# Dense FFN up and gate products as seven products of halves instead of eight; modulation weights in four slots

## The reference

```python
def swiglu(x, w1, w3, w2):
    return (jax.nn.silu(x @ w1) * (x @ w3)) @ w2
...
    cond = jax.nn.silu(c)
...
        mod = (cond @ w_mod[l] + b_mod[l])[:, None, :]
        sh_a, sc_a, g_a, sh_f, sc_f, g_f = jnp.split(mod, N_MOD, axis=-1)
...
        x = x + g_f * ((jax.nn.silu(h @ w_gate[l]) * (h @ w_up[l])) @ w_down[l])
```

## Time and profile before

| | |
|---|---|
| median of 3 runs | 2234.43 us (2232.43 to 2234.75) |
| profiled execution, its own time | 2232.85 us |
| its span | 2231.1 us |
| TensorE (PE) matmul busy | 2116.5 us, 95% |
| TensorE weight load (PEld) busy | 1525.7 us, 68% |
| DVE busy | 658.6 us, 30% |
| ACT busy | 363.8 us, 16% |

### The profile page before, as it was taken

The page is one execution under the profiler, slowest core; times in us unless marked ns, Lnnn a source line. Parts: engine busy times, 40 slices in busy tenths (PEclk is TensorE's granted clock), DMA queues, the critical chain, the costliest instruction groups (busy, mean ns, idle before and its releaser), DMA issues.

```text
span 2231.1 us, 33975 instructions
## 1 busy us (share of the span) xinstructions
PE 2116.5 (95%) x14688; PEld 1525.7 (68%) x14688; DVE 658.6 (30%) x1635; ACT 363.8 (16%) x861; POOL 83.7 (4%) x180
## 2 busy tenths in 40 slices
PE   8998999999989999998999999899999998999998
PEld 7786776777678877855643553487677757867776
DVE  1415424333334154242010000244433333440001
ACT  1312230000013122300010000133200012430000
POOL 3000000000000000020000000000000020000000
PEclk9999999999999998998999999999999999999999
DMA  8333234688563342337999999942579763224442
GB/s 254 114 96 123 95 123 151 210 274 285 173 193 105 93 139 82 123 97 248 348 313 371 345 323 364 298 133 95 177 232 306 255 183 113 96 95 151 134 149 94
DMA packets 333817, 421.23 MB, mean 189 GB/s; under 512 B 27222, under 2 KB 282148, under 8 KB 333668
## 3 DMA queue, kind: packets, MB, share of 16 engines
q1 hardware_dynamic: 312464, 352.96, 49.1%
q0 software_dynamic: 13408, 50.66, 6.8%
q10 hardware_dynamic: 7796, 15.43, 2.0%
HBM read 417.90 MB, written 1.05 MB: 188 GB/s over the span
## 4 chain that ended last, share of the span: by engine, by line
PE 87%; DVE 4%; ACT 3%; issue 2%; DMA 2%; ACTq 1%; POOL 0%; DVEq 0%; POOLq 0%
PE psum L1255 31%; PE psum L1372 10%; PE psum L1262 9%; PE psum L1273 9%; PE psum L1432 5%; PE psum L1889 3%; PE psum L1502 2%; PE psum L1673 2%; PE psum L1291 2%; PE psum L1361 1%; PE psum L1700 1%; PE psum L1445 1%; DVE arena L2061 1%; ACTq L635 1%; DMA arena<-in_w_mod 1%
## 5 line engine op out<-in xcount | busy, mean ns | idle before, releaser
L1255 PE MATMUL psum<-xT,ring 128*128 128x256 f32 x3520 | 786.4, 384 | 3.9 <-ACT small L758 2.1
L1255 PEld LDWEIGHTS psum<-xT,ring 128*128 128x128 f32 x3520 | 672.5, 192 | 118.9 <-issue 20.5
L1273 PE MATMUL psum<-ring,arena 128*128 128x512 f32 x528 | 232.8, 594 | 0.0
L1262 PE MATMUL psum<-ring,xT 128*128 128x256 f32 (+2 forms) x960 | 205.5, 373 | 11.8 <-DVE arena L2300 4.4
L1262 PEld LDWEIGHTS psum<-ring,xT 128*128 128x128 f32 x960 | 174.4, 194 | 39.9 <-DVE arena L2300 5.7
L1273 PEld LDWEIGHTS psum<-ring,arena 128*128 128x128 f32 x528 | 100.3, 191 | 114.9 <-issue 112.5
L2072 DVE TENSOR_TENSOR arena<-arena,psum 128x512 f32<-128x512 f32 x33 | 22.7, 687 | 407.4 <-PE psum L1255 235.0
L2061 DVE SCALAR_TENSOR_TENSOR arena<-arena,cond 128x256 f32<-128x256 f32 x336 | 135.0, 478 | 0.0
L1372 PE MATMUL psum<-ring,arena 128*32 128x256 f32 x2304 | 126.9, 379 | 0.7 <-DVE arena L2144 0.7
L667 ACT ACTIVATE arena<-psum 128x512 f32<-128x512 f32 x33 | 19.7, 597 | 578.2 <-PE psum L1255 571.9
L1372 PEld LDWEIGHTS psum<-ring,arena 128*32 128x32 f32 x2304 | 74.6, 110 | 51.3 <-issue 3.4
(11 more groups left out here) (392 smaller groups left out, 1865.5 us busy)
## 6 DMA issues: line engine op xcount, KB each, us to landing
ring<-in_w_in SPq DMA_DIRECT2D x80, 1024.0 KB, 5.4
ring<-in_exp_w SPq DMA_DIRECT2D x312, 256.0 KB, 6.0
arena<-in_w_mod POOLq DMA_DIRECT2D x48, 1024.0 KB, 10.1
ring<-in_ffn_w SPq DMA_DIRECT2D x33, 1024.0 KB, 6.1
arena<-in_exp_w SPq DMA_DIRECT2D x120, 256.0 KB, 6.8
ring<-in_w_gate SPq DMA_DIRECT2D x22, 1024.0 KB, 7.7
ring<-in_w_up SPq DMA_DIRECT2D x22, 1024.0 KB, 10.1
ring<-in_w_down SPq DMA_DIRECT2D x22, 1024.0 KB, 5.1
```

The source lines that it names most:

```text
L1255: ins = pe.matmul(dst, w[:, k * 256 + c0:k * 256 + c0 + m], act_t[:, k, :], start=(k == 0), stop=(k == KT - 1))
L1262: ins = pe.matmul(dst, act_t[:, k, t * P:t * P + P], w[:, k * 256 + c0:k * 256 + c0 + n], start=(k == 0), stop=(k == KT - 1))
L1273: ins = pe.matmul(psum[:, 4 + 2 * t + h, :], gT[:, s % 3, f * 256 + t * P:f * 256 + t * P + P], w2[:, f * D + h * 512:f * D + h * 512 + 51 ...
```

## The change

**The products.** In steps 1 to 10 of every dense FFN `xT` is cut into four quarters (channel half x token tile) and each of `w1`, `w3` into two channel halves. The outputs h1 and h3 of both token tiles are then a 2x2 times 2x2 product of blocks. It is made by seven products instead of eight (`product`: 8 matmuls with 128 moving tokens each), of which five take sums or differences. `token_sums` makes four sums of quarters of `xT` once per FFN (`xsum`, in the space of `oT`); `weight_sums` makes four sums of halves of `w1` and `w3` per step, one step ahead, on DVE (one overwrites half of the `w3` unit in the ring). The products are put together on DVE by four additions (C11, a half-width one, C22, C21) in `hh`, with one copy of the first product on ACT; then come Silu and the multiplication as before. The `down` products are unchanged.

**The modulation.** Four slots instead of three; a load waits for the unit four before. DVE's operations are cut into 19 pieces of about 10 operations, two pieces in a step (behind C21 and behind g), the last behind g of step 9. `add_mod` is one piece that stands after token tile 0's last `down` and ahead of tile 1's.

**Elsewhere.** `angles` moves up on DVE to behind the last merged block ahead of the residual; the three Sin move up on ACT accordingly.

```diff
+FIRST_BANK, PAIR_BANK, SIDE_BANK, LAST_BANK = 2, 3, 0, 1
...
+        mod_slots = [modw[:, i, :] for i in range(3)] + [view(SLOT, at=8192 - SLOT)]
...
                 for j in range(MOD_UNITS):
-                    if j >= 3:
-                        pool.wait_ge(*ready("dve", "mod", l, j - 3))
+                    if j >= 4:
+                        pool.wait_ge(*ready("dve", "mod", l, j - 4))
...
             def dense(key):
-                for s in range(FFN_STEPS):
-                    act.wait_ge(*ready("pe_job", "h1", *key, s))
+                act.wait_ge(*ready("pe_job", "h1", *key, 0))
+                step(act.activation(hh[:, 0:2, :], two(psum[:, 0, :]), ACT.Silu), "silu", *key, 0)
+                for s in range(1, FFN_STEPS):
+                    act.wait_ge(*ready("pe_job", "P1", *key, s))
                     if s >= 2:
-                        act.wait_ge(*ready("dve", "g", *key, s - 2))
-                    step(act.activation(sil[:, s % 2, :], psum[:, (2 * s) % 4, :], ACT.Silu), "silu", *key, s)
+                        act.wait_ge(*ready("dve", "C11", *key, s - 1))
+                    step(act.copy(part[:], psum[:, FIRST_BANK, 0:UNIT_FF]), "P1", *key, s)
+                    act.wait_ge(*ready("dve", "C21", *key, s))
+                    step(act.activation(hh[:, 0:2, :], hh[:, 0:2, :], ACT.Silu), "silu", *key, s)
...
+            def product(bank, half, weights, tokens):
+
+                for f in range(2):
+                    dst = psum[:, bank, half * 256 + f * P:half * 256 + f * P + P]
+                    for k in range(4):
+                        ins = pe.matmul(dst, weights[:, k, f * P:f * P + P], tokens[:, k, :],
+                                        start=(k == 0), stop=(k == 3))
+                return ins
...
+                    w1, w3 = [unit(key, w, s).rearrange("p (k c) -> p k c", k=KT) for w in ("w1", "w3")]
+                    if s >= 2:
+                        pe.wait_ge(*ready("act", "P1", *key, s - 1))
+                    job(product(FIRST_BANK, 0, w1[:, 0:4, :], x11), "P1", *key, s)
+                    if s >= 2:
+                        pe.wait_ge(*ready("dve", "C11", *key, s - 1))
+                    product(PAIR_BANK, 0, w1[:, 4:8, :], x21)
+                    pe.wait_ge(*ready("dve", "xsums", *key))
+                    pe.wait_ge(*ready("dve", "wsums", key, s))
+                    job(product(PAIR_BANK, 1, wsum2, xsum[:, 1]), "P26", *key, s)
+                    used(key, "w1", s)
...
+                    product(SIDE_BANK, 1, w3[:, 0:4, :], xsum[:, 2])
+                    job(product(SIDE_BANK, 0, wsum1, xsum[:, 0]), "P75", *key, s)
+                    pe.wait_ge(*(ready("dve", "C21", *key, s - 1) if s >= 2 else ready("dve", "g", *key, 0)))
+                    product(LAST_BANK, 1, w3[:, 4:8, :], xsum[:, 3])
+                    job(product(LAST_BANK, 0, wsum4, x22), "P34", *key, s)
+                    used(key, "w3", s)
+                    if s < last:
+                        downed(down(key, s - 1, w2), key, s - 1)
+                    else:
+                        down(key, s - 1, w2, (0,))
+                    w2_old, w2 = w2, unit(key, "w2", s)
+                job(down(key, last, w2, (0,)), "sum", *key)
                 if key in MOD_HOME:
-                    add_mod(MOD_HOME[key], 0)
...
+                    add_mod(MOD_HOME[key])
+                downed(down(key, last - 1, w2_old, (1,)), key, last - 1)
+                downed(down(key, last, w2, (1,)), key, last)
...
+            def weight_sums(key, s):
+
+                for w in ("w1", "w3"):
+                    dve.wait_ge(*ready("slot%d" % ring_place[key, w, s], "unit", key, w, s))
+                w1, w3 = [ring[:, ring_place[key, w, s], :].rearrange("p (k c) -> p k c", k=KT) for w in ("w1", "w3")]
+                if s >= 2:
+                    dve.wait_ge(*ready("pe_job", "P75", *key, s - 1))
+                step(dve.tensor_tensor(wsum1[:], w3[:, 0:4, :], w3[:, 4:8, :], ALU.add))
+                free(dve.tensor_tensor(w3[:, 0:4, :], w1[:, 0:4, :], w3[:, 0:4, :], ALU.subtract))
+                step(dve.tensor_tensor(wsum2[:], wsum1[:], w1[:, 0:4, :], ALU.subtract))
+                if s >= 2:
+                    dve.wait_ge(*ready("pe_job", "P34", *key, s - 1))
+                free(dve.tensor_tensor(wsum4[:], w1[:, 4:8, :], wsum2[:], ALU.subtract), "wsums", key, s)
...
+                for s in range(1, FFN_STEPS):
+                    dve.wait_ge(*ready("act", "P1", *key, s))
+                    dve.wait_ge(*ready("pe_job", "P26", *key, s))
...
+                    if s + 1 < FFN_STEPS:
+                        weight_sums(key, s + 1)
+                    dve.wait_ge(*ready("pe_job", "P34", *key, s))
+                    step(dve.tensor_tensor(hh[:, 1:3, :], hh[:, 1:3, :], two(psum[:, LAST_BANK, :]), ALU.add),
+                         "C21", *key, s)
+                    if s + 1 < FFN_STEPS:
+                        some_modulation(2 * s - 1)
                     dve.wait_ge(*ready("act", "silu", *key, s))
...
+                    some_modulation(2 * s)
```

More of the change, by code:

```diff
@@ L923, in _ @@
                     step(act.activation(zb[:, :, c, :], zb[:, :, c, :], ACT.Sigmoid), "sig", l, c)
+                if l == 0:
+                    act.wait_ge(*ready("dve", "angles"))
+                    for side, sign in ((0, -1.0), (1, 1.0)):
+                        step(act.activation(trig_sin[:, :, side, :], two(ang[:, 1, :]), ACT.Sin, scale=sign))
+                    step(act.activation(trig_cos[:], two(ang[:, 2, :]), ACT.Sin), "trig")
                 warm_roots("ln1", l)
@@ L934, in _ @@
                     step(act.activation(e2, e2, ACT.Exp), "router_exp")
-                if l == 0:
-                    act.wait_ge(*ready("dve", "angles"))
-                    for side, sign in ((0, -1.0), (1, 1.0)):
-                        step(act.activation(trig_sin[:, :, side, :], two(ang[:, 1, :]), ACT.Sin, scale=sign))
-                    step(act.activation(trig_cos[:], two(ang[:, 2, :]), ACT.Sin), "trig")
                 if l == 0:
@@ new lines, in token_sums @@
+            def token_sums(key):
+                x11, x12, x21, x22 = [xT[:, 4 * (i // 2):4 * (i // 2) + 4, P * (i % 2):P * (i % 2) + P]
+                                      for i in range(4)]
+                if key[0] == "ffn1":
+                    dve.wait_ge(*ready("act", "xt", "f1", 0, 1))
+                else:
+                    dve.wait_ge(*ready("act", "modulated", "ffn", key[1], 1))
+                    dve.wait_ge(*ready("dve", "modulated", "ffn", key[1], 1))
+                step(dve.tensor_tensor(xsum[:, 0], x12, x11, ALU.subtract))
+                free(dve.tensor_tensor(xsum[:, 2], x22, x12, ALU.subtract))
+                step(dve.tensor_tensor(xsum[:, 1], x22, xsum[:, 0], ALU.subtract))
+                free(dve.tensor_tensor(xsum[:, 3], x21, xsum[:, 1], ALU.subtract), "xsums", *key)
```

130 lines of the change are left out of this document (67 added, 63 removed).

## The result

| | before | after |
|---|---|---|
| median, same chip | 2234.75 us (5 runs, 2232.43 to 2242.83) | 2226.88 us (5 runs, 2224.74 to 2229.54) |
| ratio | | 0.9949, 95% interval 0.9929 to 0.9969 |
| profiled execution, its own time | 2232.85 us | 2229.54 us |
| its span, mean granted clock | 2231.1 us, 0.981 | 2227.8 us, 0.971 |

The change makes the kernel faster by 0.5%, where 0.7% was forecast. The median lies 9 us above the forecast of 2218 and inside the range of 2195 to 2228, near its end.

What follows compares the result with a forecast made beforehand. TensorE's matmuls, busy 95% of the span, were taken as the bound. 34.7 - 20.0 - 3.3 + 5.1 = 16.5 us off 2232.85 gave 2216.4, plus 1.58 for a median: 2218 us, range 2195 to 2228.

Steps and rivals of the forecast that it cites:

- products, three FFNs: Steps 1 to 10 of each dense FFN: 56 short matmuls replace 32 of 256 columns, saving 34.7 us.
- gaps in the steps: Two FFNs with modulation: TensorE waits for late weight sums and g, costing 20.0 us, bounds 0 and 26.
- clock behind these gaps: After two of the four stalls the granted clock falls, 1.64 us each: 3.3 us lost, bounds 0 and 6.6.
- the ends: Ends of the first two FFNs, up to the next stage's transposes: 2.1 and 3.0 us gained, 5.1 together.
- Two pairs in one step: In step 3, 4 MB of modulation makes w3 land at 22.7 us; TensorE waits 4.6 us, twice per FFN.
- At no cost: In the FFN steps DVE's load, token sums, ACT's copy and Silu, and moved angles cost nothing.
- No stalls: Rival: the two pairs' loads fall apart or yield to the ring's; 39.8 us gained, 2194.6 us, chance 0.32.
- stalls of 2 us: If DMA queues share the rate equally, the second pair delays w3 by about half; stalls 2 us, not 4.6.
- More stalls: Rival: two pairs meet the weights in every third step and gaps cost clock; 2232 to 2236 us, chance 0.08.
- Slower by a new bound: Rival: weights land late in every step with modulation; 2278 us if w3 always lands at 22.7, chance 0.07.

Runs made afterwards that it cites:

- run 9: The changed kernel measured a second time, unaltered, against the kernel before: 2225.07 us against 2237.98 us, ratio 0.9940.
- Experiment 1: Changed kernel with modulation loads held back until the w3 unit of the step behind the pair's first operation has landed: 2209.81 us, ratio 0.9871 to the kernel before.
- experiment 2: Changed kernel loading only the first four of 24 modulation units per layer, DVE's work kept: 2202.4 us, ratio 0.9824 to the kernel before.
- experiment 5: Changed kernel with modulation cut into pieces of 16, then 4 and 5 in turn, so pairs begin one step apart: 2207.89 us, ratio 0.9846 to the kernel before.
- experiment 3: Changed kernel with all modulation loads but only the first and last of DVE's eight multiply-adds per unit: one run of 2222.39 us.
- experiment 7: Changed kernel with modulation cut 14, then 4 and 5, its loads held behind w3, and add_mod between tile 0's last down groups: 2190.01 us, ratio 0.9776 to the kernel before.
- experiments 6: Changed kernel with add_mod between token tile 0's two last down groups instead of behind them: 2215.77 us, ratio 0.9887 to the kernel before.
- experiment 4: Changed kernel with three slots for modulation units instead of four: 2282.55 us, ratio 1.0192 to the kernel before.

## Why the prediction was right, and where it was off

The sum was 16.5 us. Against the second profile of the kernel before, which has the changed kernel's clock outside the FFNs, the span fell by 13.0 (2240.8 to 2227.8), and by 12.9 in the medians of run 9. Step by step:

| us | forecast | measured |
|---|---|---|
| products, three FFNs | +34.7 | +39.3 (30 x 1.31) |
| gaps in the steps | -20.0 | -20.1 |
| clock behind these gaps | -3.3 | -6.1 |
| the ends | +5.1 | +3.2 |
| clock behind the ends | not counted | -4.1 |
| sum | 16.5 | 12.2 |

The number came close partly by luck: the products gave 4.6 us more than forecast, the clock and the ends took 8.8 more, and within the gaps step 4 was shorter and step 8 longer than said. The steps that were mis-sized are these.

- **The products** were mis-sized, for the better. 12.51 us for 56 is 0.2234 us each, not 0.2266 or 0.2256. The 7.25 us of step 0 in the earlier trace rows run from the first matmul after an idle of 1.16, so what a start behind an idle costs was spread over only 32 matmuls; a group of 16 records behind a gap takes 1.86 us start to start (508.08), 1.79 within the stream. The rate within a long stream was 1.2% better, and over 1680 matmuls that is 4.6 us. The 81 ns of the Trainium skill (TensorE: Matmul & The Clock Gate, section Back-to-back issue gap) would have been 324 ns a matmul by the prediction's working; the trace has 223.4, so the page's figure does not hold for this stream. Short matmuls did not slow down over 56 in a row.
- **Two pairs in one step** was right in place and, in the sum, in size: the large gaps are in steps 4 and 8 of both FFNs. Their sum is 2.75 + 0.36 + 5.33 + 0.29 + 1.11 = 9.8 in the first and 0.27 + 2.28 + 5.44 + 1.23 + 1.11 = 10.3 in the second (0.36, 0.29 and 0.27 are small gaps in steps 6, 10 and 3), where 10.0 was said. Experiments 1, 2 and 5 show the cause, and experiment 3 that less work on DVE does not take it away. The inner course was only partly as told. In step 4 the last link was DVE's queue, which stood 6.6 us for modulation where some 4 were said; in step 8 it was `w3` itself, 25 us after its step's start where 22.7 was said. TensorE waited for it at the step's start and not only ahead of the third product, since its program asks for `w1` and `w3` both before the first product. Doubling the delay of one pair was 2 us too little: seven units of 1.05 MB in a step of 19.4 us would be 379 GB/s, more than the 320 and 367 that the first two windows below show at a DMA share of 0.96 and 1.02. So the load of two pairs does not end within its step, and by the packet counts above it is the ring's that ends last.
- **The clock.** Two falls of 1.64 were taken; three came in the steps, of 1.69, 1.80 and 2.63, within the bound of 6.6. But the two in step 8 hide a wait. There the weight sums for the third product ended at 552.42 + 1.22 = 553.64 us, and TensorE came to it at 554.19. At full clock it would have come at 548.82 + 3.57 = 552.39 and waited for DVE until about 553.8 (at 467.12 it started 0.15 after the sums' end). So that fall cost about 0.4 us and not 1.80, and by the same working on the second FFN's rows 1.2 and not 2.63 (estimates from these starts). Experiment 1 shows the case: behind 2.37 us idle nothing fell (3.81 us at 540.73), and 1.16 of waiting for DVE followed. So the clock's own price in the steps is an estimated 3.3 us, and the late `w3` costs some 2.8 more than the row of gaps says, 22.9: the term that was mis-sized is the landing of `w3` in step 7, at 25 us in place of 22.7. Windows of the changed kernel (as in experiment 7; the last three figures are granted clock, DMA share and GB/s): the step with two pairs, the start of the next with its gap, then behind this gap, and last in step 8 when the clock was back:

```profile
441.00:460.00 19.00, 19.00 (x128) 15.38 (x128) 12.38 (x25) 0.89 (x2) 3.51 (x4) 1.00 0.96 320
...
460.00:466.00 6.00, 4.37 (x34) 3.73 (x32) 5.83 (x8) 0.00 (x0) 0.00 (x0) 1.00 1.02 367
...
467.00:471.00 4.00, 3.88 (x20) 3.92 (x21) 3.96 (x10) 0.89 (x2) 0.00 (x0) 0.57 1.10 349
...
557.00:560.00 3.00, 3.00 (x30) 3.00 (x28) 3.00 (x8) 0.00 (x0) 0.00 (x0) 1.00 0.00 0
```

- **The ends.** From the last product's end to the transposes the first FFN took 623.12 - 602.40 = 20.7, less the 1.1 for `g` 19.6, as said. The second took 22.0, less 1.1 20.9, where 19.0 was said: TensorE waited 3.59 for the four DMAs. It now reaches that place sooner, while the modulation's rows start later. What was put at nothing, without a reason, is the clock behind these waits: 10.05 for 7.41 us (2.6) and 3.50 for 2.05 (1.45). In experiments 6 and 7, which take the waits away, both are gone.
- **At no cost**, as said: DVE's load, the token sums, ACT's copies, `angles`. In experiment 2, which has them all, TensorE waits in no step.
- **The level.** The range's end, 2228, takes the ends at their full +5.1; with every term at its worst bound the sum is 2.1 and the time 2232, so the range was too narrow for its own bounds. Of the 9 us between 2218 and 2226.88 the terms explain 4.3. The rest is of the size by which runs of one kernel differ: the forecast, and the first set too, had the kernel before at 2234.4 and 2234.75, the later sets at 2237.98 to 2241.5. The changed kernel came out at 2226.88 and 2225.07, so the gain was 7.9 us in the one set and 12.9 in the other; 12.2 lies within the intervals of both ratios.
- **The rivals.** "No stalls", worth 39.8, is what the kernel does once the stalls are taken away: experiment 7 gained 51 us, the 39.3 of the products and nearly all of the rest at the ends. By the Trainium skill (DMA: Bandwidth & Descriptors, section Queues, rings and completion order) an engine goes round its queues packet by packet. The trace agrees: 287 packets of either queue from 532 to 536 us. What failed is the prediction's step from there to equal rates and stalls of 2 us: equal turns of packets of 3.9 and 1.0 KB are 1.11 and 0.28 MB.
- *More stalls* was priced at 62 less 39.8, which is 22 us slower than before; the 2232 to 2236 beside it rest on an overlap that was not worked out.
- "Slower by a new bound" is not what this change does, but it is what it does with three slots (experiment 4).

What stays open: why the clock falls behind some gaps and not others, and why the falls outside the FFNs come in one run and not in the next.

## What to carry to other kernels

Count the bytes that must land in each step, not on average: 258 GB/s over the FFN was harmless, seven units in one step were not, and the same bytes started one pair a step apart gave back most of it. Where two queues load at once, compare their packets: here they took equal turns, and the queue with packets four times as large got four times the rate. When work is cut into pieces, cut it by where its loads begin and not by equal size. And before a forecast of under 1% is set against one profile, look at its granted clock: it moved this kernel by 20 us with nothing changed.

## What the runs showed of the hardware that was not expected

- Short matmuls pay almost nothing in a steady stream: a matmul took 0.2234 us with 128 moving columns, half of the 0.432 (13.82 us for 32) with 256, plus 3%.
- Two DMA queues that load at once moved equal numbers of packets and not of bytes: 1.11 MB to 0.28 in 4 us, with packets of 3.9 and 1.0 KB.
- A gap can cost more than its idle time, and the length alone does not tell. Behind 2.12 us idle a group of 3.73 us took 5.44 (experiment 5, 1782.26), while behind 2.28 us in the changed kernel nothing fell (1679.23). Inside the steps, gaps of 0.37 to 1.23 us cost no clock in the rows above.
- The clock's falls far from any change came at the same places in different kernels, and in one run out of two: 0.83 in the window from 240 to 260 us in one profile of the kernel before and in one of the changed kernel, 0.91 in the other profile of the kernel before.
